# Expert weights in longer runs, a strided moving operand, and activations turned by VectorE

## What is computed

```python
D_MODEL, SEQ, D_FF, N_EXPERTS, TOP_K = 1024, 256, 2816, 8, 2

def swiglu(h, w_gate, w_up, w_down):
    return (jax.nn.silu(h @ w_gate) * (h @ w_up)) @ w_down

def moe_swiglu(h, w_router, w_gate, w_up, w_down):
    ...
    for e in range(N_EXPERTS):
        out = out + comb[..., e:e + 1] * swiglu(h, w_gate[e], w_up[e], w_down[e])
    return out
```

## Time and profile before

| | |
|---|---|
| median of three runs | 1698.43 us |
| profiled execution: its own time, its span | 1700.35 us, 1698.6 us |
| TensorE busy | 1605.9 us, 95% |
| VectorE, ScalarE, GpSimd busy | 752.3, 542.6, 164.0 us |
| read from HBM | 421.62 MB |
| largest entries of the chain that ended last | L3392 16%, L3438 8%, down pieces in DMA 10% |

### The profile page before, as it was taken

One profiled execution on the slowest core, in us unless ns is written; L12 is line 12 of the kernel. 1 busy time (PEld: TensorE's weight loads), 2 busy tenths in 40 slices (PEclk: granted clock), 3 DMA queues, 4 the chain that ended last, 5 costly groups with the idle time before them and its releaser, 6 DMA issues.

```text
span 1698.6 us, 40371 instructions
## 1 busy us (share of the span) xinstructions
PE 1605.9 (95%) x18179; PEld 1189.2 (70%) x18179; DVE 752.3 (44%) x1450; ACT 542.6 (32%) x909; POOL 164.0 (10%) x239
## 2 busy tenths in 40 slices
PE   8999999999999999999999999989999879999975
PEld 5788877788888888787778856655766545666643
DVE  5799678765555499967867410000000000000002
ACT  5235665566343433556646400000000000000001
POOL 7340002000000225000200010000000000000010
PEclk9999999999999999999999899999999999999998
DMA  9434533357462544453125679999999999999995
GB/s 275 147 131 170 192 109 121 139 177 243 157 214 99 167 149 140 158 198 129 71 78 184 260 292 399 408 399 409 399 408 391 406 383 407 388 408 394 408 400 202
DMA packets 170995, 433.50 MB, mean 255 GB/s; under 512 B 19516, under 2 KB 47816, under 8 KB 170824
## 3 DMA queue, kind: packets, MB, share of 16 engines
q1 hardware_dynamic: 164552, 419.45, 66.1%
q0 software_dynamic: 3408, 9.27, 1.6%
q10 hardware_dynamic: 2864, 2.23, 0.4%
HBM read 421.62 MB, written 9.31 MB: 254 GB/s over the span
## 4 chain that ended last, share of the span: by engine, by line
PE 72%; DMA 13%; DVE 5%; ACT 4%; SPq 2%; issue 1%; POOL 1%; ACTq 0%; DVEq 0%
PE banks L3392 16%; PE banks L3438 8%; DMA ring<-in_moe_w_down 6%; PE banks L2743 5%; DMA past_ring<-in_moe_w_down 4%; PE banks L3216 4%; PE banks L3218 4%; PE banks L3217 4%; PE banks L2768 3%; PE banks L2772 3%; PE banks L2769 3%; PE banks L2676 3%; PE banks L2680 3%; PE banks L2677 3%; PE banks L2652 2%; DMA past_ring<-in_moe_w_gate 2%
## 5 line engine op out<-in xcount | busy, mean ns | idle before, releaser
L2543 DVE SCALAR_TENSOR_TENSOR phase<-phase,banks 128x768 f32<-128x768 f32 (+3 forms) x24 | 19.1, 796 | 576.0 <-ACT phase L1621 576.0
L3392 PE MATMUL banks<-ring,phase 128*32 128x256 f32 (+1 forms) x4480 | 232.6, 363 | 15.2 <-DMA ring<-in_moe_w_up 9.8
L3392 PEld LDWEIGHTS banks<-ring,phase 128*32 128x32 f32 x4480 | 145.1, 110 | 96.0 <-DMA ring<-in_moe_w_up 14.1
L3392 PE MATMUL banks<-past_ring,phase 128*32 128x256 f32 (+1 forms) x3584 | 191.6, 371 | 12.2 <-DMA past_ring<-in_moe_w_up 6.6
L3392 PEld LDWEIGHTS banks<-past_ring,phase 128*32 128x32 f32 x3584 | 120.8, 113 | 76.8 <-issue 9.9
L3438 PE MATMUL banks<-ring,phase 128*32 128x256 f32 x2288 | 130.9, 383 | 9.6 <-DMA ring<-in_moe_w_down 8.5
L1621 ACT ACTIVATE phase<-banks 128x768 f32<-128x768 f32 (+3 forms) x24 | 16.4, 684 | 350.6 <-PE banks L3392 350.6
L3438 PEld LDWEIGHTS banks<-ring,phase 128*32 128x32 f32 x2288 | 82.4, 111 | 53.2 <-issue 9.1
L1691 DVE TENSOR_TENSOR ring_r<-ring,ring_r 128x1024 fp32r<-128x1024 f32 x71 | 84.8, 1220 | 22.6 <-ACT ring_r L1118 22.5
L1118 ACT ACTIVATE ring_r<-ring 128x1024 fp32r<-128x1024 f32 x71 | 73.9, 1057 | 53.6 <-PE banks L2769 47.1
L3438 PE MATMUL banks<-past_ring,phase 128*32 128x256 f32 x1408 | 81.7, 385 | 8.7 <-DMA past_ring<-in_moe_w_down 8.7
(11 more groups left out here) (668 smaller groups left out, 3071.2 us busy)
## 6 DMA issues: line engine op xcount, KB each, us to landing
ring<-in_w_in SPq DMA_DIRECT2D x27, 2048.0 KB, 8.0
ring<-in_moe_w_down SPq DMA_DIRECT2D x25, 2048.0 KB, 23.6
ring<-in_moe_w_gate SPq DMA_DIRECT2D x19, 2048.0 KB, 22.3
ring<-in_moe_w_up SPq DMA_DIRECT2D x18, 2048.0 KB, 25.3
past_ring<-in_moe_w_down SPq DMA_DIRECT2D x15, 2048.0 KB, 23.6
past_ring<-in_moe_w_up SPq DMA_DIRECT2D x14, 2048.0 KB, 24.0
past_ring<-in_moe_w_gate SPq DMA_DIRECT2D x13, 2048.0 KB, 22.1
ring<-in_moe_w_up SPq DMA_DIRECT2D x9, 1536.0 KB, 21.5
```

What stands on the lines that cost most here:

```text
L3392: last = mm(out[r_, g, 0:w], fx_e[n % 2][:, kk, g * GS:(g + 1) * GS], cols[:, k, j * w:(j + 1) * w], start=kk == 0 and g in opens, stop=kk ...
```

## The change

The rows of `down` are dealt to the partitions anew. In the first two chunks partition p of a piece holds the four neighbouring rows 4p to 4p + 3 of 512, one run of 16 KB; in the last chunk it holds pairs of neighbouring rows out of 256, runs of 8 KB, two in the first piece and one in the second. The inner index that meets down's partition p in block r is then no longer consecutive with p. To match it, gate's and up's moving operand takes its 32 columns per block with a step of 4 floats (2 in the last chunk) instead of side by side. Which columns quarter j holds is chosen so that a transpose of each 32 x 32 block by itself gives the stationary operand that `down` needs. So `flip` and `take_turned` go, and VectorE makes `actT_e` from `mf_act` with one block-wise transpose per chunk, behind `times_up`. The waits on `act_tr` go; the waits on `actT_ready` in gate and the two `turn_` functions become waits on `act_ready`. The gate and up pieces, their loads and their buffers stay as they are.

```diff
                     for i in range(2):
                         s, to = place_for("d", n, c, i)
-                        k0, k1 = 8 * c + 4 * i, 8 * c + (4, 8 if c < NC - 1 else 6)[i]
-                        sp.dma_start(to[:, 0:(k1 - k0) * D].rearrange("p (k n) -> p k n", n=D),
-                                     down[e][:, k0:k1, :]).then_inc(piece_full[s], 16)
+                        r, turns_ = (4, 1) if c < NC - 1 else (2, 2 - i)
+                        rows = moe_down_d[l // 2][e][c * CW[0] + i * 4 * P:c * CW[0] + i * 4 * P + r * turns_ * P, :]
+                        sp.dma_start(to[:, 0:r * turns_ * D].rearrange("p (b n) -> p b n", b=turns_),
+                                     rows.rearrange("(b p r) n -> p b (r n)", p=P, r=r)).then_inc(piece_full[s], 16)
...
-                                take_turned(n, c)
...
-                        dve.wait_ge(act_tr, base + v)
...
+                    def turn_activations(n, c):
+                        w, v = CW[c] // 4, chunk_at(n, c)
+                        dve.wait_ge(act_ready, base + v + 1)
+                        if v >= 2:
+                            dve.wait_ge(split_used, USED + used_after("d", *(divmod(v - 2, NC))))
+                        V.transpose(actT_e[v % 2].rearrange("p (g n) -> p g n", g=TG)[:, 0:tg(n), 0:w],
+                                    mf_act[:, 0:tg(n), 0:w]).then_inc(actT_ready, 1)
...
                                 times_up(n, c)
+                                turn_activations(n, c)
...
-                                pe.wait_ge(actT_ready, base + v - 1)
+                                pe.wait_ge(act_ready, base + v - 1)
...
-                            cols = arrived_piece(kind, n, c, i)[:, 0:4 * CW[c]].rearrange("p (k f) -> p k f", f=CW[c])
+                            cols = arrived_piece(kind, n, c, i)[:, 0:4 * CW[c]].rearrange(
+                                "p (k b j f r) -> p k j b r f", k=4, j=4, f=GS, r=4 if c < NC - 1 else 2)
...
-                                        last = mm(out[r_, g, 0:w], fx_e[n % 2][:, kk, g * GS:(g + 1) * GS],
-                                                  cols[:, k, j * w:(j + 1) * w], start=kk == 0 and g in opens, stop=kk == KD - 1 and g in closing)
+                                        last = mm(out[r_, g, 0:w].rearrange("p (b r f) -> p b r f", f=GS, r=4 if c < NC - 1 else 2), fx_e[n % 2][:, kk, g * GS:(g + 1) * GS],
+                                                  cols[:, k, j], start=kk == 0 and g in opens, stop=kk == KD - 1 and g in closing)
...
-                    def acts(v, c, g, k):
...
+                    def acts(v, g, k):
+
+                        return actT_e[v % 2][:, g * CQ + k * GS:g * CQ + (k + 1) * GS]
...
-                                flip(n, c)
```

More of the change, by code:

```diff
@@ L822, in expert_pieces @@
                 gate, up = (w[l // 2].rearrange("e (k p) f -> e p k f", p=P) for w in (moe_gate_d, moe_up_d))
-                down = moe_down_d[l // 2].rearrange("e (k p) n -> e p k n", p=P)
                 free_after = [multiplied(l, U_OUT + 1), multiplied(l, U_WQ), multiplied(l, U_WQ), multiplied(l, U_WQ),
@@ L1621, in gate_tanh_ @@
                         nc.scalar.activation(mf_th[:, 0:tg(n), 0:w], gate_cols(v)[:, :, 0:w], ACT.Tanh, scale=0.5).then_inc(gu_th, 1)
[L1623 to L1627, removed]
                     def one_pass(p):
@@ L3331, in turn_rows @@
                         pe.wait_ge(rows_in, 16 * (ROWS_LAID + n))
-                        pe.wait_ge(actT_ready, base + chunk_at(n - 1, 1))
+                        pe.wait_ge(act_ready, base + chunk_at(n - 1, 1))
                         for k in range(KD):
@@ L3339, in turn_weights @@
                         pe.wait_ge(matrix_ready, 2 * scatter_turn(n) + 2)
-                        pe.wait_ge(actT_ready, base + chunk_at(n, 1))
+                        pe.wait_ge(act_ready, base + chunk_at(n, 1))
                         at = (chunk_at(n, 2) % 2) * SET
@@ L3437, in product @@
                             for j, r_ in enumerate(QUADS):
-                                last = mm(out[r_, g, :], acts(v, c, g, k), w[:, k % 4, j * CQ:(j + 1) * CQ],
+                                last = mm(out[r_, g, :], acts(v, g, k), w[:, k % 4, j * CQ:(j + 1) * CQ],
                                           start=c == k == 0 and g in opens, stop=ends and k == last_k and g in closing)
```

## The result

The changed kernel takes 1931.37 us (median of 4 runs, 1928.5 to 1932.5) against 1697.76 for the kernel before beside it: a ratio of 1.1371, 95% interval 1.1356 to 1.1385. The prediction was 1693 us in a range of 1686 to 1895, so both the forecast and the range missed. What came is rival A, TensorE held up by the step of 16 bytes, but above the part of it that the range took in.

A forecast was written before the change was run, and what follows sets the result against it. DMA was taken to set the pace, with TensorE close behind. Profiled 1700.35 - 1.6 (end) - 4.0 (runs) = 1694.75, less 1.92 to the median, gave 1693 us; range 1686 to 1895, the forecast's own 1686 to 1697.

The forecast's parts named there:

- rival A: Gate and up on TensorE: the step makes TensorE the bound, 1882 us at factor 2, about 1939 at 2.2; chance 0.37.
- What bounds the kernel: Expert layer: DMA sets the pace, only just; a wide expert needs 84.6 us of TensorE beside 85.2 us of DMA.
- Part 1: End of the kernel: without flip and its copy it gains 1.6 us (1.2 to 2.05); in the stream nothing.
- Part 2: VectorE's 24 transposes: 0.955 us each, at most twice that, covered by the next chunk's pieces; cost 0.
- Part 3: Down's loads: runs of 16 and 8 KB instead of 4 KB save 4.0 us, of 0 to 5.9.
- The lines through the rows of 1 to 4 KB: Down's loads: two fits of packet time, carried on to 410 and 418 GB/s at 16 KB, 409 and 414 at 8 KB.
- The outer line: Down's loads: fit through the 1 and 4 KB packet times, 6.1 ns fixed, giving 418 GB/s at 16 KB.
- Rival C: Down's loads: long runs are slower; half of a 132 us bound gives about 1760 us; chance 0.03.
- its bound from instruction packets: Down's loads: all 16 KB runs at the 1.16 us of instruction packets would add 132 us; given little weight.
- Part 4: Gate and up on TensorE: the 16-byte step costs 0, since 0.83 ns a column leaves room above 0.45 ns.
- The bound from above: Gate and up: with VectorE's 1.62 to 1.83 ns per hopped element, TensorE's columns take 1.95 to 2.2 times as long.
- The break-even: TensorE against DMA: the step stays free to a factor of 1.35 on average, about 1.25 for two wide experts in a row.

The follow-up runs named there:

- runs_alone: The kernel before with only the loads of down changed, to runs of 16 and 8 KB: 1688.98 us, ratio 0.9947.
- quarter_stepped: step_on_vector with one of four k rows in chunks 0 and 1 stepped by 16 bytes on TensorE's read and PSUM write: 1697.34 us, ratio 0.9994.
- runs4k: The changed kernel with one row of down a partition, so 4 KB runs and no step: 1697.32 us, ratio 0.9997.
- step_on_vector: The changed kernel with TensorE reading neighbours in chunks 0 and 1 and VectorE's multiply writing the permuted order instead: 1687.54 us, ratio 0.9941.
- step_alone: The kernel before with only gate's and up's columns in chunks 0 and 1 read with a step of 4 floats: 1961.81 us, ratio 1.1555.

## Why the prediction was wrong

**What bounds the kernel: right.** runs_alone touches nothing but DMA and gains 9.2 us; quarter_stepped shows how close TensorE is behind. (The 402 to 404 GB/s were the stretches shown; others of the expert layer had 396 to 402.)

**Part 1, flip and its copy: right.** In the timeline of runs4k the last chunk's down no longer follows a flip but waits 2.71 us for its piece:

```profile
1677.90 3.66 PE L3415 MATMUL banks<-ring,phase 128*32 128x256 f32 x64 [2.71 <-DMA ring<-in_moe_w_down]
1681.35 1.94 PE L3415 MATMUL banks<-past_ring,phase 128*32 128x256 f32 x32
```

That piece was there at 1677.90, where the prediction had put 1678.1, and down ends at 1683.29 instead of 1684.67, 1.4 us earlier in these two executions, within the 1.2 to 2.05. The medians differ by 0.6 us, which the interval can't tell from nothing.

**Part 2, transposes: right.** 978 ns for 768 elements against 955 taken, and no cost in runs4k. Its view of waits does put 4.5 us before down to the transposes, but down needs the transpose of the chunk before, which ended long ahead: of the down at 1100.33 us it ended at 1073.43. Pieces arrive some 5.1 us apart there, so the wait is more likely for the piece.

**Part 3, longer runs: right in kind, too small.** The term was 4.0 us of 0 to 5.9; it measured 9.8 (runs4k to step_on_vector) and 9.2 (runs_alone). So even with the step free the kernel would have landed at 1687.5, not 1693, and inside the forecast's own range only by the margin added on its low side. The lines through the rows of 1 to 4 KB were carried on to 410 to 418 GB/s, and the stretches show 421 to 426. The outer line (6.1 ns fixed) was the better one, and still short. The estimate by the Trainium skill (DMA: Bandwidth & Descriptors, Measured; 425 GB/s) was about 9 us; on the 227.2 us of down it is rather 10.2. The trace agrees with the rate (421 and 426). Rival C, long runs slower, never came up; its bound from instruction packets had nothing to do with these.

**Part 4, the step: this is the step that failed.** "I take 0: TensorE's port shows nearly twice the rate that these matmuls ask for." The rate was real, but it was that of contiguous floats. The earlier trace rows show 0.45 ns for each of 512 neighbouring columns; four of those are one 16-byte line in 1.79 ns, the same 1.79 ns that a stepped column costs. So the row does not show that the port delivers any float in 0.45 ns. It fits a port that delivers a line in 1.8. That both matmuls meet the same limit is a reading of the equal numbers: no run steps a float32r operand. What the runs do show is the price of the float32 one. With one float used of a line, a column takes 1.79 ns against a pace of 0.83, a factor of 2.14. The bound from above, 1.95 to 2.2 from VectorE's hops, held the value; that two engines come so close was not explained, so part of this may be luck. Its case that 8 bytes are free was nearly right: 56.9 against 54.0 ns. The reading of the Trainium skill that spared this matmul, full speed meaning 0.45 ns, had put the two-hit rule aside on the strength of the same mistaken row.

**Rival A: the right mechanism, and its sum holds.** With 2.14 the prediction's own account gives 593 + 287 x 1.14 = 920 us of TensorE work and 976.2 + 12 + 920 + 13.9 = 1922 us of span; 1930.1 were measured. Of the 8 us between, the 8-byte step of the last chunks makes about 6 (40.7 to 43.0 ns a record, as under step_alone):

```profile
1893.01 5.69 PE L3394 MATMUL banks<-past_ring,phase 128*32 128x192 f32 x128
...
1904.02 10.58 PE L3415 MATMUL banks<-ring,phase 128*32 128x256 f32 x192
```

SP's gaps came as that part had listed them, the records are 114 ns apart instead of near 107, and the DMA share is under 0.9 in eight of nine stretches.

**The break-even: a slope, not a threshold.** Between "free" and "bound by TensorE" the prediction put a threshold at 1.35 on average (with the 12 us that it allows for waits; without them 704 and 593 us give 1.39) and at about 1.25 for two wide experts in a row. quarter_stepped sits at 1.29, under the first and over the second, and pays 10 us. The DMA share falls only in the second expert of each wide pair, so it is the account of the pairs that holds. No run lies below 1.25.

**Range.** Its top, 1895 us, cut through rival A between factors of 2 and 2.2, both inside the bounds that part 4 had worked out. The prediction said that it left out 0.13 above, and what came lies there. By those bounds the range had to reach 1939 to hold A.

## What to carry over

A rate measured on neighbours bounds nothing for a step: turn it into time per 16-byte line, count the lines that an element then needs, and compare that with the pace of the instruction. If a layout needs a step somewhere, put it on an engine with time to spare, or on the writing side, and not on the operand that paces the kernel: here the same permutation cost 244 us on TensorE's read (1931.4 against 1687.5) and nothing that shows on VectorE's write, which left the longer runs to give their 10 us. And when your own bounds for a rival reach beyond your range, say so at the top of the range, or widen it.

## What was unexpected

- A float32 moving operand is read at 1.79 ns per 16-byte line and stream, at a distance of 16 as of 32 bytes, and side-by-side streams do not share that limit: 114 ns a record with four streams stepped, 451 for one stream alone, which is four times 113.
- Writing a matmul's result to PSUM with a step of 16 bytes cost nothing (54.0 ns a record). VectorE's write to SBUF with hops of 128 bytes does cost: 1540 instead of 955 ns for 768 elements, 0.76 ns each, inside the 0.58 to 0.79 that the prediction had read from other rows for a hop.
- Runs beyond 4 KB still pay: from 4 to 8 KB the down loads gained some 6 us, and from 8 to 16 KB another 3 by the bytes moved (1.9 to 4.3 by the medians).
- flip, worth 1.4 us where DMA sets the pace, is worth some 30 us (29.5 by the timeline) where TensorE does.
